# First pass of a recurrent mixer layer on eight cores: scaling the W_in chunks straight into the weight ring

## The reference, cut to what matters

```
u = rmsnorm(x, norm_mix)                         # x: 16 prompts of 2048 frames, 32 streams of 32 frames, width 1024
proj = u @ w_in                                  # w_in: 1024 x 5632
xl, gl, xp, gp, ml, mp = jnp.split(proj, SPLITS, axis=-1)     # 1024, 1024, 512, 1024, 1024, 1024
xc, new_conv = causal_conv(xl, conv_s, conv_w, conv_b)
h, new_lru = rg_lru(xc, lru_s, pos0, w_rg_a, b_rg_a, w_rg_i, b_rg_i, lru_lambda)
lru_out = h * jax.nn.silu(gl)
pooled, new_pool = multi_pool(xp, pool_s, pos0)
pg = jnp.einsum('btgi,gij->btgj', pooled.reshape(B, T, N_POOL_GROUPS, POOL_GROUP), w_pool) + b_pool
pool_out = pg.reshape(B, T, D_MODEL) * pool_scale * jax.nn.silu(gp)
merged = jax.nn.sigmoid(ml) * lru_out + jax.nn.sigmoid(mp) * pool_out
x = x + merged @ w_out
gate = jax.nn.sigmoid(rmsnorm(x, norm_ple) @ w_ple_gate)
x = x + gate * (p @ w_ple)                       # then a last rmsnorm
```

## Time and profile before

| | us |
|---|---|
| median of three runs | 1426.3 |
| the three runs | 1386.77, 1426.3, 1467.9 |
| the profiled execution | 1386.53 |
| its span, slowest core (core 5) | 1385.0 |
| spans of the other cores | 1366.2 to 1384.1 |
| end of phase B of tile 0 (first group of round 1 starts) | about 298 |
| a full round after that | about 137 |

### The profile page before, as it was taken

The page is one execution under the profiler, slowest core; times in us unless marked ns, Lnnn a source line. Parts: engine busy times, 40 slices in busy tenths (PEclk is TensorE's granted clock), DMA queues, the critical chain, the costliest instruction groups (busy, mean ns, idle before and its releaser), DMA issues.

```text
span 1385.0 us, 19921 instructions; the slowest of 8 cores (1366.2 to 1385.0 us)
## 1 busy us (share of the span) xinstructions
PE 1052.1 (76%) x5185; PEld 484.6 (35%) x5185; DVE 965.3 (70%) x1405; ACT 838.5 (61%) x1319; POOL 511.0 (37%) x697
## 2 busy tenths in 40 slices
PE   1032534599899979988989889988998999897773
PEld 0010211244344434433434334434443444344451
DVE  2224667857885788678757886788578868876762
ACT  2121425539864986498539853986498648855752
POOL 1000011533464346424632354246434632472342
PEclk9985667799999999999999999999999999999887
DMA  5799978353445344544343435344544343335520
GB/s 143 238 278 281 284 251 271 120 167 119 136 132 155 119 136 131 156 119 153 106 147 120 138 122 150 116 140 130 153 121 150 100 141 111 122 112 153 168 81 37
DMA packets 111924, 208.02 MB, mean 150 GB/s; under 512 B 12273, under 2 KB 40185, under 8 KB 111813
## 3 DMA queue, kind: packets, MB, share of 16 engines
q1 hardware_dynamic: 106299, 189.15, 45.2%
q10 hardware_dynamic: 5514, 17.59, 3.1%
HBM read 177.58 MB, written 29.12 MB: 149 GB/s over the span
## 4 chain that ended last, share of the span: by engine, by line
PE 34%; DVE 24%; issue 13%; ACT 12%; DMA 11%; POOL 3%; SPq 1%; ACTq 1%; DVEq 1%; POOLq 0%
PE psum L670 22%; DMA win_bf<-u 8%; DVE wk L742 5%; PE psum L1018 4%; PE psum L981 4%; DVE xrt L1053 2%; DVE wk L806 2%; DVE wk L816 2%; DVE wk L910 2%; DVE u L528 2%; DVE xrt L985 1%; POOL xrt L1042 1%; DVE wk L906 1%; DVE wk L747 1%; PE psum L1033 1%
## 5 line engine op out<-in xcount | busy, mean ns | idle before, releaser
L670 PE MATMUL psum<-ut,wr 128*128 128x512 bf16 (+1 forms) x1600 | 347.7, 373 | 61.7 <-DMA wr<-win_bf 38.8
L670 PE MATMUL psum<-ut,extra 128*128 128x512 bf16 (+1 forms) x1568 | 348.2, 377 | 17.6 <-ACT ut L658 7.6
L670 PEld LDWEIGHTS psum<-ut,wr 128*128 128x128 bf16 x1600 | 153.9, 102 | 240.6 <-issue 89.3
L670 PEld LDWEIGHTS psum<-ut,extra 128*128 128x128 bf16 x1568 | 151.4, 101 | 198.0 <-issue 47.4
L742 DVE SCALAR_TENSOR_TENSOR wk<-xlw,cvec,wk 128x512 f32<-128x512 f32 (+1 forms) x216 | 153.7, 712 | 45.3 <-POOL xlw L709 19.7
L1018 PE MATMUL psum<-wpg,u2t 128*128 128x512 bf16 x528 | 140.5, 427 | 48.7 <-ACT u2t L1004 37.9
L622 POOL TENSOR_TENSOR stat<-stat,negh 128x1 f32<-128x1 f32 x99 | 70.8, 715 | 277.4 <-DVE stat L620 270.3
L981 PE MATMUL psum<-wout,mg 128*128 128x512 bf16 x528 | 122.7, 387 | 5.3 <-POOL mg L917 4.1
L917 POOL TENSOR_TENSOR mg<-mg,wk 128x512 bf16<-128x512 bf16 (+1 forms) x72 | 86.3, 1199 | 90.4 <-DVE wk L913 80.8
L1042 POOL TENSOR_TENSOR xrt<-xrt 128x1024 f32<-128x1024 f32 x33 | 80.9, 2452 | 88.6 <-DVE xrt L1037 84.0
L761 PE MATMUL psum<-xcb,wa 128*128 128x512 bf16 (+1 forms) x72 | 27.6, 384 | 98.9 <-DVE xcb L746 96.8
(11 more groups left out here) (112 smaller groups left out, 1829.6 us busy)
## 6 DMA issues: line engine op xcount, KB each, us to landing
wr<-win_bf SPq DMA_DIRECT2D x200, 256.0 KB, 2.8
extra<-win_bf SPq DMA_DIRECT2D x196, 256.0 KB, 2.7
xs<-xp SPq DMA_DIRECT2D x32, 512.0 KB, 5.3
xrt<-xp SPq DMA_DIRECT2D x32, 512.0 KB, 4.9
yp<-xrt ACTq DMA_DIRECT2D x32, 512.0 KB, 3.4
xrt<-w_in SPq DMA_DIRECT2D x15, 1024.0 KB, 9.5
win_bf<-u SPq DMA_DIRECT2D x44, 256.0 KB, 4.9
mg<-w_in SPq DMA_DIRECT2D x7, 1024.0 KB, 8.7
```

The source lines that it names most:

```text
L670: P.op("pe", lambda e, kc=kc: e.matmul(bank.ap[:, 0:N], lhsT=wv[:, kc, :], rhs=ut_v[:, kc, :], start=(kc == 0), stop=(kc == 7)), reads=[ws ...
```

## The change

The staging of round 0 works in single chunks instead of pairs, and VectorE writes the scaled chunk into the ring slot itself. The slot is the source of the store to `win_bf`, which later rounds still read. The read-back of round 0 is gone: `ring_load` for a position below 44 is `chunk_compute_next`. There are six staging areas of 512 KB in place of three of 1 MB. The chunks are therefore computed when `win_get` asks for them, not one pair a task, and the deferred weights begin when all 44 are done.

```
@@
     def chunk_load_next():
         i = cu["loaded"]
-        pr = PAIR_ORDER[i]
+        m = W_ORDER[i]
         hb, own = STGC[i % len(STGC)]
-        wr = [hb.buf] + (own if own[0] is not MG[1].buf else [])
-        P.dma(lambda e: e.dma_start(out=hb.ap, in_=d_w_in[0][:, pr * 256:(pr + 1) * 256].rearrange(
-            "(k p) n -> p k n", p=128)), lane=hb.buf, writes=wr)
+        P.dma(lambda e: e.dma_start(out=hb.ap, in_=d_w_in[0][:, m * 128:(m + 1) * 128].rearrange(
+            "(k p) n -> p k n", p=128)), lane=hb.buf, writes=[hb.buf])
...
-        for t_ in range(2):
-            m = 2 * pr + t_
-            ub = ubs4[cu["u"] % len(ubs4)]
-            cu["u"] += 1
-            P.op("dve", lambda e, ub=ub, t_=t_: e.tensor_tensor(
-                out=ub.ap.rearrange("p (k n) -> p k n", k=8), in0=hb.ap[:, :, t_ * 128:(t_ + 1) * 128], in1=g1b,
-                op=ALU.mult), reads=[hb.buf, CV.buf] + own, writes=[ub.buf])
-            P.dma(lambda e, ub=ub, m=m: e.dma_start(out=d_wsc[m], in_=ub.ap), lane=ub.buf, reads=[ub.buf],
-                  writes=[wsc_buf[m]])
-            chunks_done.add(m)
+        slot = RING[i % RING_N]
+        P.op("dve", lambda e: e.tensor_tensor(out=slot.ap.rearrange("p (k n) -> p k n", k=8), in0=hb.ap, in1=g1b,
+                                              op=ALU.mult), reads=[hb.buf, CV.buf] + own, writes=[slot.buf])
+        P.dma(lambda e: e.dma_start(out=d_wsc[m], in_=slot.ap), lane=slot.buf, reads=[slot.buf], writes=[wsc_buf[m]])
         cu["done"] += 1
-        if cu["loaded"] < NPAIR:
+        chunks_done.add(m)
+        if cu["loaded"] < NM:
             chunk_load_next()
...
     def ring_load(q):
         m = W_ORDER[q % NM]
-        ensure_chunk(m)
+        if q < NM:
+            assert cu["done"] == q
+            chunk_compute_next()
+            return
         slot = RING[q % RING_N]
...
     for _ in range(len(STGC)):
         chunk_load_next()
-    for _ in range(3):
-        chunk_compute_next()
...
             if r == 0:
-                if cu["done"] < NPAIR:
-                    chunk_compute_next()
-                if cu["done"] >= NPAIR and deferred_w:
+                if cu["done"] >= NM and deferred_w:
                     deferred_w.pop(0)()
```

More of the change, by code:

```diff
@@ L498, in build_program @@
     g1b = CV.ap[:, G1:G1 + 8].unsqueeze(2).to_broadcast([128, 8, 128])
[L499 to L505, removed]
+    STGC = [(T(XR[i].ap.rearrange("p (k n) -> p k n", k=8), XR[i].buf), []) for i in range(3)]
+    STGC.append((T(TGC[0].ap.rearrange("p (k n) -> p k n", k=8), TGC[0].buf), []))
+    mg1f = MG[1].ap.bitcast(F32)
+    for h in range(2):
+        STGC.append((T(mg1f[:, h * 1024:(h + 1) * 1024].rearrange("p (k n) -> p k n", k=8), P.buf("mg1st%d" % h)),
+                     [MG[1].buf]))
+    cu = {"loaded": 0, "done": 0}
     chunks_done = set()
-    NPAIR = len(PAIR_ORDER)
     def chunk_load_next():
         i = cu["loaded"]
-        pr = PAIR_ORDER[i]
+        m = W_ORDER[i]
         hb, own = STGC[i % len(STGC)]
-        wr = [hb.buf] + (own if own[0] is not MG[1].buf else [])
-        P.dma(lambda e: e.dma_start(out=hb.ap, in_=d_w_in[0][:, pr * 256:(pr + 1) * 256].rearrange(
-            "(k p) n -> p k n", p=128)), lane=hb.buf, writes=wr)
+        P.dma(lambda e: e.dma_start(out=hb.ap, in_=d_w_in[0][:, m * 128:(m + 1) * 128].rearrange(
+            "(k p) n -> p k n", p=128)), lane=hb.buf, writes=[hb.buf])
         cu["loaded"] += 1
@@ L1116, in build_program @@
         if r == 0:
-            while cu["done"] < NPAIR:
-                chunk_compute_next()
+            assert cu["done"] == NM
             while deferred_w:
```

## The result

| | before | changed |
|---|---|---|
| median of ten runs, us | 1388.4 | 1337.6 |
| ratio, 95% interval | 1 | 0.9645 (0.9619 to 0.9671) |
| the profiled execution, us | 1386.5 | 1338.4 |
| its span, us | 1385.0 | 1336.9 |

The change saves 3.55%, 49 us; the prediction was 1347, 40 us saved. The kernel before now has a median of 1388.4, close to the profiled execution on which the sum was built. The medians are of all ten executions; the ratio leaves out those in which the cores of one die ran some per cent longer at a lower granted clock.

The account below looks back on a forecast made before the run. Round 0 was taken as bound by the store's round trip and transfer time together. Fill 92, blocks 91, Q tasks 64.6 and tail 11 make 258.6 instead of 298.3, 40 less: 1386.5 - 40 = 1347 us, range 1318 to 1392.

Parts of the forecast that it names:

- first L733 (the fill): Start of round 0 up to the first elementwise work: it comes at 92 us instead of 109.2, saving 17.
- seven blocks: Round 0's channel blocks, first to eighth L733: 13 us each, 91 us instead of 138.6, saving 48.
- Q tasks: Round 0 behind the blocks: five scalings and ten deferred conversions join, adding 14 us to 50.5.
- tail: Behind the Q tasks: eight conversions ahead of round 1's L733, 6 to 14 us, adding 11.
- round 0 ends, as summed: Fill, blocks, Q tasks and tail together: 258.6 us instead of 298.3, 40 us less.
- The packets: Round 0's W_in loads: a 512-byte packet costs between 30 and 50 ns, taken as 34.
- The rival with packets at 50 ns: Small packets and VectorE at upper bounds: 1385 us, no change; chance 0.25, with all cases saving under 28 us.
- the upper is VectorE's busy share where DMA does not press ... I take the middle, 13: Channel blocks: 10.8 us of VectorE work over a 71% share gives 15.2 at most; 13 a block taken.
- the lower bound of 11.4: Channel blocks: 10.8 us of VectorE work plus 0.6 of idle time that is not DMA.
- The new wait on matmul groups: Scalings in the blocks wait right ahead of L733, which needs the same groups: costs little, under 2 us each.
- The rival of the two engines taking turns: Blocks: VectorE and the matrix engine don't overlap, 22.3 us a block, 156 in all, 1412 us; chance 0.07.
- the bound of 0 to 14: Q tasks: added time is 0 to 14 us, 14 if none of it fits into VectorE's idle 14.8.

Follow-up runs that it names:

- 17 us for the wait: Changed kernel, but a scaling again waits until the store of the scaling two before has landed: ratio 0.9770 to the kernel before, 1354 us.
- 15 for the traffic: Changed kernel plus 40 of the 44 read-backs as pure traffic that no engine waits for: ratio 0.9752 to the kernel before, 1350 us.
- with 16 buffers: Kernel before with 16 buffers for the scaled chunk instead of two, pairs and read-backs kept: ratio 0.9913, 1372 us.
- a look-ahead of 6 alone: Changed kernel with the ring filled 6 positions ahead in round 0 instead of 16: ratio 0.9650 to the kernel before.
- the fastest version: Changed kernel with the ring 8 ahead in round 0, deferred weights spread, the first try's two stalls mended: ratio 0.9477 to the kernel before, 1313.7 us.

## Why the prediction was right, point by point

| term | predicted | measured |
|---|---|---|
| first L733 (the fill) | 92 | 91.4 |
| seven blocks | 91 (13 each) | 78.9 (11.3 each) |
| Q tasks | 64.6 | 60.3 (170.3 to 230.6) |
| tail | 11 | 15.3 (19.8 us from group to L729, for 4.5) |
| round 0 ends, as summed | 258.6 | 245.9 |

The forecast of the time was 9 us too long, that of round 0 12.7 us; of the four terms the first was close, the second 12 us too dear, and the errors of the other two, 4 us each, cancel, which is luck. (One reading was off by a little: PE's digits in the first seven slices are 0 to 5, not 1 to 5. Nothing hangs on it.)

**The packets.** In 60 to 90 us of the changed kernel, and then in all of the fill:

```profile
DMA packets 11857, 7.91 MB, mean 264 GB/s; under 512 B 323, under 2 KB 10562, under 8 KB 11855
...
q1 hardware_dynamic: 11855, 7.89, 92.8%
```

```profile
DMA packets 21548, 13.65 MB, mean 256 GB/s; under 512 B 517, under 2 KB 19794, under 8 KB 21544
```

0.928 x 16 x 30 us = 445 us; less 1293 packets of 2 KB at 0.106 leaves 308 for 10,239, 30 ns each. I had taken 34. By the Trainium skill's rule of 3 cycles a packet (DMA: Bandwidth & Descriptors, "Why small descriptors are slow (HBM only)"), which I had set aside, the estimate was 27, so the measured 30 lies between it and my figure. With 30 in my sum the fill would have ended at 87. It ended at 91.4 all the same: up to then the engines moved 13.65 MB, 0.8 MB more than the 18 loads and 13 stores that I had counted: parts of the next transfers, which were already under way. That is some 3 us at 256 GB/s. So the good fit of the fill is in part luck, a packet that was too dear and too few of them. The rival with packets at 50 ns is out.

**The blocks** are the mis-sized term. The step "the upper is VectorE's busy share where DMA does not press ... I take the middle, 13" fails: the blocks stand at the lower bound of 11.4, with 11.3, of which VectorE is busy 10.6. The 71% came from the Q tasks, where VectorE waits for other engines in a way the blocks don't. The sum of VectorE's own work, 10.8, plus the 0.6 of idle time that was not DMA, was the better forecast by itself. This is 12 us, nearly the whole error of round 0.

**The new wait on matmul groups** cost nothing that shows: no scaling of the changed kernel has idle time put down to PE, as the order of the gate matmuls had suggested. The rival of the two engines taking turns is out: the blocks took 79 us, not 156. One sign was off: PE's waits for `xcb` were to be well below 10 us each; at the end of the blocks one was 13.3, in the tail 11.3.

**The Q tasks** were 4 us shorter, inside the bound of 0 to 14.

**The tail** was 4 us longer. Eight conversions, five of them with a wait for their load of 2.4, 2.3, 0.5, 1.3 and 2.8 us, run from 234.5 to 250.5: 16 us, where the sum had 14 at most and made 11 of them for PE's own work. That work doesn't shorten the way to L729, whose input from ScalarE was there at 235. For PE it was more than the sum had: three groups, the output projection and three more groups, 14 us and not 5. So PE, seen by itself, lost 12 us: the first gate matmul of round 1 comes 25.9 us after the first group (256.5 after 230.6), where before it was 13.8.

**The cause** was told too simply. The prediction let the store's round trip and the transfer time bound the loop together, without a price for either. The runs price them: 17 us for the wait, 15 for the traffic, and they add. The remaining 19 (12 to 26 by the interval) are open, with SP standing for stores as a candidate that no run tried. So the time was right without the cause being known in full. What the prediction's sum did right was to leave the causes alone and count, for each stretch, what the engine that stays busiest has to do.

## What to carry to other kernels

Where a wait and traffic bound a stage together, forecast the stage by the work of the engine that is next in line (instructions times their durations, plus the idle time that has another reason), and not by a share taken from another stage. Taking away the wait that ends last shows nothing of what stands right behind it: with 16 buffers the blocks kept their length. Making the start of a pipeline earlier pays only if the loads of the work behind it are asked for earlier too: a look-ahead of 6 alone moved the start by 30 us and the end by none, and with the late loads spread it was part of the fastest version. A copy of the data that has just been made on chip should be used from where it lies; the store to HBM can run behind it.

## What the runs showed of the hardware that I had not expected

Where tensor operations of VectorE and GpSimd lie beside each other in time, one of the two can take about twice as long. The changed kernel, VectorE and then GpSimd:

```profile
186.89 1.22 DVE L523 TENSOR_TENSOR extra<-mg,cvec 128x1024 bf16<-128x1024 f32 x1
188.02 2.29 DVE L523 TENSOR_TENSOR extra<-xrt,cvec 128x1024 bf16<-128x1024 f32 x1
```

```profile
186.91 2.31 POOL L824 TENSOR_TENSOR mg<-wk 128x512 bf16<-128x512 f32 x1
```

The same scaling takes 1.22 or 2.29 us; GpSimd's operation takes 1.26 at the shortest and 2.31 here. The first scaling starts with GpSimd's operation and keeps its 1.22 us; GpSimd's ends 1.1 us after that scaling, nearly its own length; and the second scaling ends 1.1 us after GpSimd's. By these times each of the three seems to have done its work after the one before it had ended. What holds them wasn't tried. In the blocks it happens too, with VectorE's scan as the long one:

```profile
116.98 2.24 DVE L812 TENSOR_TENSOR_SCAN wk<-wk 128x512 f32<-128x512 f32 x1
```

```profile
116.88 1.26 POOL L824 TENSOR_TENSOR mg<-wk 128x512 bf16<-128x512 f32 x1
```

It can make work that is moved from the fill to the Q tasks dearer than its price in the fill.
